# One 2 MB weight transfer cut into five: 96 rows and four times eight rows, on one Trainium2 core

## The reference, cut to what matters

```python
grp_probs = softmax(xt @ w_grp + b_grp); p_grp, g_idx = top_k(grp_probs, 1)
w_e, e_idx = top_k(softmax(sel_logits), 2)          # 2 of the 8 experts of the chosen group
for gi in range(4):                                 # 4 groups of 8 experts
    hdn = silu(xt @ w_gate[gi]) * (xt @ w_up[gi])   # (1024 x 512) each, float32
    y = y + (hdn * comb) @ w_down[gi]               # (512 x 1024)
out = rmsnorm(h + y)
```

## Time and profile before

| what | value |
|---|---|
| time, median of 3 runs | 782.75 us (781.74 to 785.69) |
| time of the profiled execution | 782.64 us |
| its span, first to last instruction | 780.9 us |
| TensorE busy | 749.0 us, 96% of the span |
| DMA engines, mean rate over the span | 309 GB/s |
| the same in the expert stage | about 427 GB/s |
| granted TensorE clock, mean | 0.997 |

### The profile page before, as it was taken

How to read it: one execution, slowest core, us unless ns; L and a number is a source line. 1 busy time by engine, 2 the same in 40 slices (tenths; PEclk the granted TensorE clock), 3 DMA queues, 4 the chain that set the end, 5 groups by cost and what they waited for, 6 DMA issues and landing times.

```text
span 780.9 us, 16087 instructions
## 1 busy us (share of the span) xinstructions
PE 749.0 (96%) x6517; PEld 535.7 (69%) x6517; DVE 324.8 (42%) x794; ACT 312.7 (40%) x632; POOL 123.9 (16%) x208
## 2 busy tenths in 40 slices
PE   8999999999999999899999999999999999998895
PEld 7989989998999988655555555555556455454452
DVE  4894787688675855812211311221113113012012
ACT  7876678676584744712211121212122211211113
POOL 7463242224433640000000000000000000000000
PEclk9999999999999999999999999999999999999999
DMA  8545555554754568899999999999999999999992
GB/s 210 139 126 142 154 141 135 134 149 110 183 142 123 145 202 309 379 378 430 427 427 428 427 427 427 427 428 427 427 426 427 427 426 428 429 427 426 428 408 92
DMA packets 81106, 241.08 MB, mean 309 GB/s; under 512 B 6914, under 2 KB 65395, under 8 KB 68995
## 3 DMA queue, kind: packets, MB, share of 16 engines
q1 hardware_dynamic: 80722, 239.19, 80.6%
q10 hardware_dynamic: 304, 0.79, 0.4%
HBM read 238.92 MB, written 1.05 MB: 307 GB/s over the span
## 4 chain that ended last, share of the span: by engine, by line
PE 79%; DMA 11%; issue 4%; DVE 3%; ACT 1%; SPq 0%; DVEq 0%; ACTq 0%
PE banks L2139 23%; PE banks L1794 21%; PE banks L2195 12%; DMA ring<-in_expert_w_up_dram 10%; PE banks L2071 3%; PE banks L2150 3%; PE banks L1989 2%; PE banks L1913 1%; PE banks L2171 1%; PE banks L1926 1%; PE banks L1974 1%; PE banks L1930 1%; PE banks L1917 1%; DMA room<-in_w_in_dram 1%; PE banks L1951 1%
## 5 line engine op out<-in xcount | busy, mean ns | idle before, releaser
L2139 PE MATMUL banks<-ring,bench 128*64 128x256 f32 x2048 | 240.0, 388 | 11.7 <-DMA ring<-in_expert_w_up_dram 7.1
L2139 PEld LDWEIGHTS banks<-ring,bench 128*64 128x64 f32 x2048 | 146.5, 134 | 112.6 <-issue 23.7
L1794 PE MATMUL banks<-rounded 128*128 128x256 f32 (+3 forms) x1344 | 198.8, 294 | 2.3 <-DVE desk L1448 1.4
L1794 PEld LDWEIGHTS banks<-rounded 128*128 128x128 f32 (+1 forms) x1344 | 171.1, 188 | 6.3 <-issue 1.5
L1693 DVE TENSOR_TENSOR bench<-banks,bench 128x256 f32<-128x256 f32 x32 | 13.6, 425 | 263.0 <-PE banks L2139 171.6
L2195 PE MATMUL banks<-ring,bench 128*64 128x512 f32 x512 | 116.9, 598 | 0.5 <-ACT bench L1077 0.5
L1088 ACT ACTIVATE ysb<-banks 64x512 f32<-64x512 f32 x63 | 37.3, 592 | 147.1 <-PE banks L2195 146.3
L2195 PEld LDWEIGHTS banks<-ring,bench 128*64 128x64 f32 x512 | 33.8, 136 | 63.3 <-issue 60.2
L856 ACT ACTIVATE rounded<-room 128x1024 fp32r<-128x1024 f32 x64 | 67.5, 1054 | 21.6 <-PE banks L1794 15.0
L1312 DVE TENSOR_TENSOR rounded<-room,rounded 128x1024 fp32r<-128x1024 f32 x49 | 66.3, 1353 | 14.7 <-ACT rounded L856 13.6
L1077 ACT ACTIVATE bench<-banks 128x256 f32<-128x256 f32 x32 | 12.3, 385 | 147.5 <-PE banks L2171 147.5
(11 more groups left out here) (309 smaller groups left out, 858.6 us busy)
## 6 DMA issues: line engine op xcount, KB each, us to landing
ring<-in_expert_w_gate_dram SPq DMA_DIRECT2D x30, 2048.0 KB, 28.4
ring<-in_expert_w_down_dram SPq DMA_DIRECT2D x30, 2048.0 KB, 27.2
ring<-in_expert_w_up_dram SPq DMA_DIRECT2D x29, 2048.0 KB, 28.6
room<-in_w_in_dram SPq DMA_DIRECT2D x56, 512.0 KB, 4.2
ring<-in_expert_w_gate_dram SPq DMA_DIRECT2D x8, 512.0 KB, 6.0
ring<-in_expert_w_up_dram SPq DMA_DIRECT2D x8, 512.0 KB, 6.3
ring<-in_expert_w_down_dram SPq DMA_DIRECT2D x8, 512.0 KB, 18.8
room<-in_w_out_dram SPq DMA_DIRECT2D x8, 512.0 KB, 4.4
```

What stands on the lines that cost most here:

```text
L1794: ins = T.matmul(o, a, b[:, k, lo_at:L], start=(k == 0 and n == 0), stop=(k == KT - 1 and n == 2))
L2139: ins = T.matmul(pb[5 + c][half * 64:half * 64 + SLOTS, 0:256], xgT[:, q % ROOMS, kt, j * SLOTS:(j + 1) * SLOTS], w[:, kt, half], start=(k ...
```

## The change

The gate matrix of expert 31, the last one, is no longer loaded by one transfer of 128 rows but by five that follow each other on the same queue: partitions 0 to 95, then 96 to 103, 104 to 111, 112 to 119 and 120 to 127. Source, destination, bytes and the wait ahead of them are as before. All five add 16 to the same semaphore, so the count that TensorE waits for is 64 higher.

```diff
+SPLIT = (EXPERTS - 1, 0)
+SPLIT_ROWS = (96, 8, 8, 8, 8)
@@ load_chunk
+            elif (e, c) == SPLIT:
+                at = 0
+                for rows in SPLIT_ROWS:
+                    eng.dma_start(dst[at:at + rows], src[at:at + rows]).then_inc(S(f"w_land{3 * (e % RINGS) + c}"), 16)
+                    at += rows
             else:
                 eng.dma_start(dst, src).then_inc(S(f"w_land{3 * (e % RINGS) + c}"), 16)
@@ landed
-                    pe.wait_ge(S(f"w_land{3 * (e % RINGS) + c}"), 16 * (loads + quarters + (e // RINGS + 1)))
+                    extra = len(SPLIT_ROWS) - 1
+                    split = extra * ps if (e % RINGS, c) == (SPLIT[0] % RINGS, SPLIT[1]) else 0
+                    if (e, c) == SPLIT:
+                        split += extra
+                    pe.wait_ge(S(f"w_land{3 * (e % RINGS) + c}"), 16 * (loads + quarters + split + (e // RINGS + 1)))
```

## The result

The changed kernel took 797.96 us in the median (795.77 to 801.80, 6 runs) against 783.60 us of the kernel before beside it. The ratio that the comparison gives is 1.0171, 95% interval 1.0139 to 1.0203, or +13.4 us; the two medians by themselves lie 14.4 us apart, within that interval, since runs of one kernel scatter by 5 us (told of at the end). The forecast was +4.9 us, its range ended at 791.0. The direction was right, the size was not, and the measured time lies outside the range.

The account below looks back on a forecast made before the run. Late in the expert stage TensorE was taken to follow weight landings, with 0.5 us slack at expert 31's gate. Landing 5.4 us later less 0.5 gave +4.9: 782.64 + 4.9 = 787.5, median 787.6 us; range 782.6 to 791.0.

Parts of the forecast that it names:

- What bounds the kernel, and the frame: Late expert stage: TensorE follows weight landings; expert 31's gate weights landing D later end the kernel D - 0.5 later.
- Spread over the engines, 1.23 us: Four eight-row transfers: if they share the same eight engines, these carry 10 rows instead of 8, +1.23 us; alternating, +0.
- How fast few rows go: Cut gate transfer: neighbouring rows share a destination limit; four small transfers take 6.1 us, the middle of 2.46 and 9.83.
- D = 5.4: Forecast later landing of expert 31's gate weights: 3.7 + 6.1 - 4.9 = 4.9 us, plus 0.5 for the 96 rows.
- D = 8.6: Upper end for the gate weights' delay: 96 rows at full rate, then four small transfers one after the other, 9.83 us.
- What is late next: nothing: Behind expert 31's gate: up and down weights land before they are wanted, so nothing adds up, 0 us.
- The clock is not at stake: TensorE in the expert stage: clock stays at 1.00, as in earlier windows with idle time; no cost.
- D - 0.5: Kernel's later end: the gate weights' landing delay less 0.5 us of slack, forecast 4.9 us.
- B (convoy): Four small transfers: engines catch up and go through all together, 8.6 us delay or a little more, 790.8 up; chance 0.10.
- A: Cut gate transfer: the spread hides it, only row count matters; end moves 0 to 0.7 us, 782.6 to 783.4; chance 0.28.
- D: As a rival: SyncE held so long that expert 31's down parts come late, 785 to 788 us; chance 0.03.

Follow-up runs that it names:

- the sets with 8 to 64 rows: Kernel before with the block left out, only loading equal transfers of 16 KB rows: 54 GB/s for 8 neighbours, 204 GB/s for 32 neighbours.
- the tidy queue: Kernel before with the block left out: sets of seven 2 MB transfers, engines not put apart; fourth transfer in five parts 48.42 us, whole 37.26 us.
- 96+32: One matrix loaded as transfers of 96 and 32 rows; for expert 31's gate in the kernel before: 795.52 us, ratio 1.0138.

## Why the prediction was wrong, point by point

*What bounds the kernel, and the frame.* Right. The gate weights of expert 31 had 0.5 us of slack, and every us that they came later came out at the end. Also right: five issues and four more additions to a semaphore are free (five by columns, 0.9985, though SyncE was held 15.5 us by them there and 3.1 us in the changed kernel), and the down parts are no bound.

*Spread over the engines, 1.23 us.* The count of engines was right (share 0.50). The term may be too small by itself: next to a harmless 32-row pattern four eights cost 4.6 us of lag, but what of that is the count of engines and what the groups is open.

*How fast few rows go.* This is the step that failed. The mechanism was read rightly from the earlier trace rows, half rate for 32 neighbours, and the sets with 8 to 64 rows confirm it. Its application failed at three places. First, I let it act on the four small transfers (6.1 us) and took the 96 rows as nearly whole (3.7 us and 0.5). Measured, 96 rows alone run at 227 GB/s, 6.9 us and not 3.7, and in a full queue their price was 7.6 us where the sum has 4.2. The eights were 8.3 us where the sum has 6.1. These two differences, 3.4 and 2.2 us, are the whole way from D = 5.4 to the 11.1 or 11.2 of the tidy queue. In the kernel most of the loss is there with a plain rest of 32 rows: 10.5 of 12.1. Second, I took D = 8.6 as the upper bound, from rates of the parts alone. Alone the five parts cost just that, 8.7, but this is luck: the 96 rows were slower than the bound had them, and the parts overlapped where it had them one after the other. And the full queue widens it to 11.2 and the kernel to 12.1. Third, the distance between the engines was my reason to go *below* the upper bound, since engines apart would not crowd. It is the other way for 96+32: amid whole transfers 4.8, with engines apart 8.6; for the five parts it made little difference (11.2 and 11.6). The reason by theory 1, which fits the late landing of the transfer ahead but was not shown engine by engine: while one engine is at its cut rows, another is still at the transfer before or already at the one behind, and both of them are slowed.

*What is late next: nothing.* Wrong. The transfer ahead, expert 30's down weights, took 5.7 us longer from issue to landing than before (46.4 against 40.7), and TensorE waited 4.2 us for it. That wait is not a loss by itself, as the gate weights were later still, but it brought the low clock.

*The clock is not at stake.* Wrong by 1.4 us. Waits of 4.2 and 6.0 us were longer than any idle time in the earlier trace rows (at most 0.84 us in a window of 5), and the granted clock fell to 0.50.

In numbers: predicted D - 0.5 = 4.9. Measured in the profiled executions 12.1 of lag, -0.4 from the start of expert 30's up, +1.4 of clock: 13.1. Of the rivals, B (convoy) was nearest in its number, with "8.6 or a little more"; it had 0.10. Its mechanism, engines that catch up and then go in step, is not what the runs show: putting engines apart beforehand did not make the loss smaller. A is refuted, D did not occur.

Left open: which rows a DMA engine carries in a transfer of 96 rows, and so why spreading the eights by step 4 bought nothing beside them, why sixteen eights cost so little, and why four transfers of 32 with step 4 cost nothing. Theory 1 had these wrong or only half right; it is a good account of rates and of where the loss grows, and not yet one of its size.

## What to carry to other kernels

When DMA engines are busy without a pause, cut a transfer by columns and keep its 128 partitions; if it has to be by rows, four transfers of 32 rows with a step of 4 were free, and transfers of neighbouring rows or of eight rows were not. Price such a cut at the whole queue: a transfer issued before it landed late too. For 96+32 the rates alone give 6.9 + 2.6 - 4.9 = 4.6 us, about what it cost in a tidy queue (4.8); in this kernel it was 6 to 11, more the further the DMA engines had drifted apart. Ask of each slack how small it is: 0.5 us was all that stood between this transfer and the end.

## What the runs showed of the hardware

A transfer of 96 of 128 partitions runs at 227 GB/s, though all 16 engines are busy, and four transfers of 32 partitions with a step of 4 run in a full queue as fast as one of 128 (37.24 us against 37.26).

The granted clock also halves in the mixers, while TensorE is busy without a gap, in some executions and not in others (in 4 of the 14 profiled ones of whole kernels its mean from 60 to 70 us is 0.50 to 0.67, in seven 1.00). In the profiled execution of the kernel with 96 rows and four eights with step 4:

```profile
56.00:60.00 4.00, 4.00 (x62) 3.57 (x59) 3.06 (x9) 1.73 (x6) 2.83 (x3) 0.58 1.00 235
60.00:70.00 10.00, 10.00 (x80) 9.36 (x80) 1.35 (x6) 2.87 (x6) 5.47 (x9) 0.50 0.35 73
```

Its first expert began at 331.94 us and not at 327.29, and in the other three at 331.6 to 333.6. Runs of the kernel before show the same in their mean granted clock: those of 786.7 to 788.0 us have 0.987 to 0.990, those below 785 us 0.993 to 0.999. So this goes with the 5 us of scatter between runs of one kernel (781 to 788 before, 796 to 802 after), and it is why the lag within a trace was used beside the medians. What brings the clock down there is not shown.
